# A streaming encoder layer: recurrence inputs between two attention projections, one scaling for both tiles, and the residual kept on chip

## What is computed

```python
h   = LayerNorm_in(x)
P   = h @ w_in          # [RWKV-7 r | k | v | w-lora | a-lora | g-lora] [diff-attn q | k | v]
m   = concat(RWKV7_group(P_rw), DiffAttn_group(P_da)) @ w_out
h   = LayerNorm_1(alpha*h + m)
h   = LayerNorm_2(alpha*h + PEER(h))
# PEER, per block of 128 frames: top 16 keys of two halves, top 16 of their sums, then
u = take(u_tab, idx); act = gelu(einsum('thed,td->the', u, xb))
v = take(v_tab, idx); out = einsum('the,thed->td', gate * act, v)
# a head of attention ends with
o = o * rsqrt(mean(o*o) + eps) * da_subln_g * (1 - lam_init)
```

## Time and profile before

| | |
|---|---|
| median of 3 runs | 4598.03 us (4596.55 to 4604.55) |
| profiled execution, its own time | 4561.83 us |
| its span, first to last instruction | 4560.0 us |
| busy in the span | PE 58%, DVE 56%, POOL 52%, PEld 33%, ACT 16% |
| moved by DMA | 1335.83 MB, 293 GB/s over the span |
| chain that ended last | PE 23%, DVE 22%, POOL 19%, DMA 13%, issue 12% |

### The profile page before, as it was taken

One profiled execution on the slowest core, in us unless ns is written; L12 is line 12 of the kernel. 1 busy time (PEld: TensorE's weight loads), 2 busy tenths in 40 slices (PEclk: granted clock), 3 DMA queues, 4 the chain that ended last, 5 costly groups with the idle time before them and its releaser, 6 DMA issues.

```text
span 4560.0 us, 49804 instructions
## 1 busy us (share of the span) xinstructions
PE 2627.3 (58%) x18687; PEld 1514.2 (33%) x18687; DVE 2574.5 (56%) x5971; ACT 723.9 (16%) x1806; POOL 2365.5 (52%) x2204
## 2 busy tenths in 40 slices
PE   6767356665735666665636776667345544374345
PEld 4546344433502333334303443345112222140001
DVE  3332987756875545656955554657844546573411
ACT  3332023320101122220001222211001111000000
POOL 0000035556465555556556564565666666667665
PEclk8778677777857778667767787868565666665668
DMA  3112267889888788789789888798898998999997
GB/s 119 40 55 89 85 250 252 287 303 365 339 310 331 292 310 309 286 299 367 296 321 366 315 289 294 290 359 344 300 350 330 367 364 329 370 366 334 371 369 304
DMA packets 374663, 1335.83 MB, mean 293 GB/s; under 512 B 40764, under 2 KB 73816, under 8 KB 364184
## 3 DMA queue, kind: packets, MB, share of 16 engines
q0 software_dynamic: 315888, 1150.17, 67.8%
q1 hardware_dynamic: 58536, 182.48, 10.7%
HBM read 1312.29 MB, written 20.20 MB: 292 GB/s over the span
## 4 chain that ended last, share of the span: by engine, by line
PE 23%; DVE 22%; POOL 19%; DMA 13%; issue 12%; another core or an unknown queue 7%; ACT 4%; DVEq 0%; ACTq 0%; SPq 0%; POOLq 0%
POOL ring_u L728 10%; POOL ring_v L728 9%; DMA ring_v<-in_peer_v,idx_t 8%; PE pm L1031 7%; PE pm L1045 6%; DVE ring_u L1388 6%; PE pacc L1073 5%; DMA ring_u<-in_peer_u,idx 4%; DVE arena L1639 1%; DVE arena L1642 1%; DVE arena L1640 1%; PE pm L1256 1%; DVE arena L1641 1%; DVE arena L1638 1%
## 5 line engine op out<-in xcount | busy, mean ns | idle before, releaser
L728 POOL DMA_INDIRECT ring_u<-in_peer_u,idx x1088 | 1196.7, 1100 | 875.9 <-DVE dots L1388 564.0
L1388 DVE CUSTOM_DVE_ANT_0 ring_u<-ring_u,h 128x1024 f32<-128x1024 f32 x1088 | 1297.9, 1224 | 606.0 <-DMA ring_u<-in_peer_u,idx 534.6
L728 POOL DMA_INDIRECT ring_v<-in_peer_v,idx_t x1032 | 1102.1, 1068 | 718.4 <-PE pacc L1073 400.8
L1073 PE MATMUL pacc<-ring_v,spread_w 128*32 128x512 f32 x4128 | 834.0, 892 | 997.1 <-DMA ring_v<-in_peer_v,idx_t 884.4
L1073 PEld LDWEIGHTS pacc<-ring_v,spread_w 128*32 128x32 f32 x4128 | 141.1, 137 | 1385.8 <-issue 1367.4
L1031 PE MATMUL pm<-hT,wts 128*128 128x256 f32 (+1 forms) x2400 | 544.5, 388 | 57.5 <-SPq L654 26.8
L1045 PE MATMUL pm<-arena 64*64 64x64 f32 (+1 forms) x6256 | 388.7, 266 | 287.9 <-issue 90.8
L1031 PEld LDWEIGHTS pm<-hT,wts 128*128 128x128 f32 x2400 | 454.6, 210 | 198.1 <-issue 97.4
L1045 PEld LDWEIGHTS pm<-arena 64*64 64x64 f32 x6256 | 323.9, 167 | 447.5 <-issue 191.0
L771 POOL DMA_DIRECT2D h<-h_scratch x10 | 5.9, 596 | 551.2 <-DVE gates L1628 551.2
L1031 PE MATMUL pm<-wts,hT 128*128 128x384 f32 (+1 forms) x576 | 194.4, 496 | 0.0
(11 more groups left out here) (226 smaller groups left out, 2827.1 us busy)
## 6 DMA issues: line engine op xcount, KB each, us to landing
wts<-in_sets SPq DMA_DIRECT2D x75, 1536.0 KB
ring_u<-in_peer_u,idx POOLq DMA_INDIRECT x1088
ring_v<-in_peer_v,idx_t POOLq DMA_INDIRECT x1032
wts<-in_sets SPq DMA_DIRECT2D x10, 1024.0 KB
h_scratch<-arena SPq DMA_DIRECT2D x16, 512.0 KB, 4.2
arena<-in_subkeys SPq DMA_DIRECT2D x5, 1024.0 KB
arena<-in_x_prompt SPq DMA_DIRECT2D x8, 512.0 KB, 11.2
out<-arena SPq DMA_DIRECT2D x64, 64.0 KB
```

Of the source, the lines that this page charges most:

```text
L728: pool.indirect_dma_start(out=out, out_offset=None, in_=table, in_offset=bass.IndirectOffsetOnAxis(ap=index.bitcast(U32), axis=0)).then_in ...
L1073: x = pe.matmul(pacc[out, c, :], spread_w[:, blocks % 2, quad, place % EIGHTH, :], row[:, c * 512:(c + 1) * 512], start=(place == 0), stop ...
L1388: x = v.tensor_tensor_reduce(ring_u[:, row, :], ring_u[:, row, :], h1[:, g % 3, :], 1.0, 0.0, ALU.mult, ALU.add, dots[:, slot:slot + 1])
```

## The change

**Order in a pair.** The attention's qkv step is cut in two, one per tile. The first stands behind the recurrence's raw step, the second behind decay, and rope behind grams; the other attention steps are spread over the rest of the pair:

```diff
+        qkv = [0, 2][:s.tiles] + [3]
...
-        places = [0, 1, 2, 3] + [3 + (late - 3) * (i + 1) // (len(a) - 4) for i in range(len(a) - 4)]
+        rest = len(a) - len(qkv)
+        places = qkv + [3 + (late - 3) * (i + 1) // rest for i in range(rest)]
...
-        steps = [("qkv", 4, 0.5), ("rope", 1, 1.5)]
+        steps = [("qkv", 4 / s.tiles, 0.5 / s.tiles)] * s.tiles + [("rope", 1, 1.5)]
```

```diff
+            def raw_row(s, j, x, bank):
+
+                k = set_number("rwkv", s, j)
+                pe.wait_ge(S[f"w{k % 2}"], weights_in(k))
+                dense(pm[:, bank, 0:s.width], lambda n: column(k, x)[:, n, :], lambda n: hT[:, n, 0:s.width]).then_inc(S["raw_full"], 1)
...
+                        elif j + 1 < NJ:
+                            raw_row(s, j + 1, *RAW[0])
                         yield "mean"
                         tl.next(S["ysq_ready"])
                         pe.matmul(pm[:, 1, 0:w], mean2[:, :], sq[:, 0:w], start=True, stop=True).then_inc(S["var_full"], 1)
                         leave(pe, "pe")
+                        if not s.last and j + 1 < NJ:
+                            raw_row(s, j + 1, *RAW[1])
                         yield "variance"
...
+                        tl.next(S["ysd"])
+                        if j + 1 < NJ:
+                            raw_row(s, j + 1, *RAW[2])
```

**Both tiles' outputs together.** The root mean squares, the scaling, the turn and the copy are made once for both tiles at the end of the head; PE waits at tile 1 for `o_read`, no longer for the turned and copied output of tile 0:

```diff
-            act.activation(rms[0:r], ss[0:r], ACT.Sqrt, bias=eps_ln[0:r, :], scale=1.0 / P).then_inc(S["rms_ready"], 1)
...
+                        act.wait_ge(S["o_read"], attn_tiles(s, j) + s.tiles)
+                        act.activation(rms[0:r, 0:s.tiles], ss[0:r, 0:s.tiles], ACT.Sqrt, bias=eps_ln[0:r, :], scale=1.0 / P).then_inc(S["rms_ready"], 1)
+                        yield "scale"
```

```diff
-                                    x = dense(pm[0:s.rows, 2 * t + n // 4, (n % 4) * P:(n % 4 + 1) * P], lambda k: mixT[:, k, sl(s, t)],
-                                              lambda k: column(k0, n % 3)[:, k, :])
+                                    out = pm[0:s.rows, 2 * t + n // 4, (n % 4) * P:(n % 4 + 1) * P]
+                                    dense(out, lambda k: mixT[:, k, sl(s, t)], lambda k: column(k0, n % 3)[:, k, :], True)
+                                    x = pe.matmul(out, hT[:, n, sl(s, t)], scaled[:, :], start=False, stop=True)
```

More of the change, by code:

```diff
@@ L430, in build @@
         xt = carve(NCH, CH)
-        p1s = carve(HD)
-        us = carve(HD)
-        s_out = carve(HD)
+        p1s, us, s_out = (rkk[:, i * HD:(i + 1) * HD] for i in range(3))
         keysT = carve(SEQ)
@@ L643, in _ @@
                             sp.dma_start(ln2[:, i, :], ins[name][0].partition_broadcast(P)).then_inc(S["late_in"], 16)
-                    for t in range(s.tiles):
-                        tl.next(S["h_ready"])
-                        sp.dma_start(h_d[t * P:t * P + s.rows, :], x_in[0:s.rows, t, :]).then_inc(S["h_stored"], 16)
-                    tl.next(S["h_stored"], 16 * s.tiles)
                     sp.sem_inc(S["bar_sp"], 1)
@@ L695, in _ @@
                         load_set(base + i + 2)
-                    for t in range(s.tiles):
-                        tl.next(S["h_ready"])
-                        g = s.first_tile + t
-                        sp.dma_start(h1_d[g * P:g * P + s.rows, :], x1[0:s.rows, t, :]).then_inc(S["h1_stored"], 16)
-                    tl.next(S["h1_stored"], 16 * s.tiles)
+                    if s.sample:
+                        sp.wait_ge(S["h_ready"], 2 * len(TILES))
+                        sp.dma_start(h1[s.rows:2 * s.rows, s.first_tile % 4, :], h1[0:s.rows, s.first_tile % 4, :]).then_inc(S["h1_twin"], 16)
                 elif kind == "query":
@@ L759, in store @@
                 r = slice(seg.start + t * P, seg.start + t * P + seg.rows)
-                pool.dma_start((y_s if seg.sample else y_p)[0, r, :], h1[0:seg.rows, g % 3, :]).then_inc(S["y_stored"], 16)
+                pool.dma_start((y_s if seg.sample else y_p)[0, r, :], h1[0:seg.rows, g % 4, :]).then_inc(S["y_stored"], 16)
             for kind, g, arg in order:
@@ L845, in mixing @@
                             yield "tile"
+                        if s.n > 0:
+                            for t in range(SEGMENTS[s.n - 1].tiles):
+                                turned(SEGMENTS[s.n - 1], t)
                         for x in range(2):
@@ L1024, in _, with dense @@
             pe.wait_ge(S["consts"], 1)
-            pe.wait_ge(S["const_in"], 16)
+            pe.wait_ge(S["const_in"], 32)
             pe.sem_inc(S["bar_pe"], 1)
-            def dense(out, lhs, rhs):
+            def dense(out, lhs, rhs, more=False):
                 for k in range(KT):
-                    x = pe.matmul(out, lhs(k), rhs(k), start=(k == 0), stop=(k == KT - 1))
+                    x = pe.matmul(out, lhs(k), rhs(k), start=(k == 0), stop=(k == KT - 1 and not more))
                 return x
@@ L1258, in mixing @@
                             yield "probs"
-                            tl.next(S["o_ready"])
-                            pe.transpose(pm[:, 4, P:P + r], o_s[0:r], ident[0:r, 0:r]).then_inc(S["oT_full"], 1)
-                            yield "out"
+                        tl.next(S["o_read"])
+                        yield "scale"
+                        tl.next(S["o_ready"])
+                        for t in range(s.tiles):
+                            x = pe.transpose(pm[:, 4, P + t * P:P + t * P + r], qk[0:r, t, 0:P], ident[0:r, 0:r])
+                        x.then_inc(S["oT_full"], 1)
+                        yield "out"
                         tl.next(S["oT_read"])
@@ L1520, in mixing @@
                         enter(v, "dve", kind, s, j)
-                        yield "qkv"
+                        for t in range(s.tiles):
+                            yield "qkv"
                         for t in range(s.tiles):
```

197 lines of the change are left out of this document (103 added, 94 removed).

## The result

The changed kernel takes **4445.57 us** (median of 4 runs, 4432.29 to 4459.47) against 4601.29 us (4 runs, 4596.55 to 4604.60): a ratio of 0.9663, 95% interval 0.9631 to 0.9694. That is 156 us less; the forecast was 219 less, 4380 us. The profiled execution of the changed kernel is the slowest of its four (4459.47 us, span 4457.4), that of before was faster than all its timed runs. So the two traces differ by 103 us only. The same kernel run again in another job gave 0.9669 (0.9626 to 0.9712), with a profiled execution of 4405.86 us, so two rounds, 800 to 950 us together, differ by up to 27 us between two profiles of one kernel (rounds 0 and 1: 833 and 806). I read segment 0, which repeats within 0.2 us, from single traces, and all stages with gathers from both profiles and from the medians.

What follows compares the result with a forecast made beforehand. Mixing was taken to hold the gathers back in rounds 2 to 5, with segment 0 uncovered. Segment 0's 67 us, 39, 53 and 53 for segments 1 to 3 and 7 for the sample make 219: 4598 to 4379 us, range 4300 to 4520.

Steps and rivals of the forecast that it cites:

- The front, 15 us for each transition: Segment 0, from one pair's tail to the next pair's last product before the Gram matrices: 15 us less, bounds 11 to 17.
- the clock's rival: Raw rows and projections cut into pieces run at the lower clock; 4.2 us a pair come back, 4464 us; chance 0.13.
- Pair 0, 12 us: Segment 0's first pair: rows start earlier and decays no longer wait for both tiles' q, k, v; 12 us less.
- Project, 2 us longer: Segment 0's projection: 16 more matmuls of 0.29 us, two fewer DVE additions of 1.22 us; 2 us longer.
- One scaling and the tables, 3 us a pair: Pairs of two tiles: three fewer ACT table loads and one scaling round trip less; 3 us a pair, 0 to 4.5.
- some tenths: Front of a pair: rotations, now behind the products and partly beside the Gram matmuls, give back some tenths of a us.
- The share of 0.66 for loaded pairs: Pairs beside gathers: 0.66 of a chain's cut shows, so 18 us become 12 a pair, bounds 0 and 18.
- that is what the gathers can do: Round 8, gathers only: DMA 98% busy at 373 GB/s, taken as what the gathers can do.
- gathers hide the front: Rival: only segment 0 and the saved bytes show, 67 + 8 us, giving 4523 us; chance 0.14.
- The full cut: Rival: all 18 us show in each loaded pair of two tiles, 299 us in all, giving 4299 us; chance 0.12.
- PE's queue as the bound: Rival: raw rows ahead of v pieces in PE's list delay them, 148 us lost, giving 4671 us; chance 0.05.
- Scratch tensors, 2 us a round: Stores and loads of about 18 MB go, 2.1 MB a round; 2 us a round less where DMA is the bound.

Runs made afterwards that it cites:

- the short raw rows: Changed kernel with raw rows late and, in segments 1 to 4, one matmul instead of eight per raw row: 4399.01 us, 0.9644 of the kernel before.
- The places: Changed kernel with the attention's steps put back in their old places, both tiles' q, k, v in one step: 0.984 of the kernel before.
- halved pieces: Changed kernel with each ring piece of u rows given back to POOL in two halves: 3984.54 us, 0.9361 of the kernel before on that chip.

## Why the prediction came out as it did

The sign and the range were right, and the time was 66 us too low, 4380 for 4445.57. Segment 0 gave more than I had put down and the rest about half: 156 measured, less 78 in segment 0, leaves 78 where I had 152. That the total came within 66 us is in part luck: 11 us too little in segment 0 stand against 74 too much beside the gathers.

**The front, 15 us for each transition: right.** From the mean's matmul to the last product the three fell by 16.2, 16.4 and 15.7 us. The first raw row took some 5 us at a granted clock that averaged 0.55 from 99.0 to 104.5, the next two 7.17 together at 1.00; I had 5.5 and 6.8:

```profile
99.00:104.50 5.50, 4.92 (x18) 3.90 (x15) 0.84 (x2) 0.60 (x2) 0.00 (x0) 0.55 0.00 0
106.00:114.00 8.00, 7.89 (x38) 6.30 (x36) 6.01 (x13) 1.54 (x4) 0.00 (x0) 1.00 0.00 0
```

So the clock's rival didn't come: one row of three ran mostly at 1.2 GHz, as a part of it had before (0.68), and the projections after it took 5.32 us a tile, nearly as before (10.48 for both). Over the span the granted clock was 0.736 after 0.726.

**Pair 0, 12 us: 15.3,** its last product at 61.3 instead of 76.6. **Project, 2 us longer: 2.1,** from the last mixT of segment 0 to the list, 174.3 after 172.2.

**One scaling and the tables, 3 us a pair: two sizes that cancel.** From the last product to the mean's matmul the four pairs of segment 0 fell by 4.3, 3.7, 5.5 and 3.0 us, 16.5 where I had 12, nearly as if the term were right. But with each tile scaled by itself this stretch is 43.7 us in pair 1, where it is 36.5 with the change and was 40.2 before. One scaling is thus worth 7.2 there (5.6 to 7.2 in the four pairs), more than my upper bound of 4.5, and the rest of the change gives 3.5 back there, for which I had "some tenths". What I hadn't costed is that PE at tile 1 no longer waits until tile 0's output is scaled, turned and copied; that this makes the difference isn't tested apart from the tables. Of the load itself the rows show 1.283 us and no idle time behind it: in the transition above the load that begins at 120.78 is over when the square root starts at 122.07. The drain of the Trainium skill, page "ScalarE: Activation LUTs", section "What ACT_TABLE_LOAD costs", is not seen in this trace. Segment 0 in all: 67 forecast; 48 for the transitions, 15 for pair 0, 17 for the four stretches behind the products, less 2 for the projection, make the 78 measured.

**The share of 0.66 for loaded pairs: the term that was too large.** It came from segment 2's pairs against the sample's. That difference holds other things than PE's work: one tile instead of two, with DVE busy 254 us instead of 317 and ACT 73 instead of 132. The direct test, the short raw rows, takes PE work alone off the front of each loaded pair and finds about a quarter; and early raw rows in these segments are worth nothing that shows. The places, which do pay there (80 - 28 = 52 us by the medians, some 4 a loaded pair), and one scaling (58 - 27 = 31) pay by something else than the length of the front, if they pay: both numbers are uncertain by 25 us and more. By the traces the pairs of segment 2 fell from 588 to 560 and 552 us, those of segment 3 from 586 to 581 and 568, where I had 48 less in each: 12 a pair became 1 to 9. Rows for the two segments in the changed kernel, against the 588 us of the earlier trace rows:

```profile
1394.00:1954.00 560.00, 373.58 (x3121) 208.40 (x3120) 314.61 (x620) 114.12 (x299) 331.75 (x303) 0.79 0.84 311
2340.00:2921.00 581.00, 395.90 (x3185) 222.42 (x3185) 321.30 (x621) 119.94 (x303) 330.28 (x305) 0.77 0.83 306
```

**Behind it a wrong premise: "that is what the gathers can do".** I had read 373 GB/s in round 8 as the limit of DMA, and 830 of 986 us as what the bytes need. The bytes don't set the rounds: halved, the rounds stay. In round 8 POOL's 192 gathers and the gaps between them fill some 250 of its 280 us; rounds 2 to 5 are 256 gathers, 320 us at least and some 355 at their mean, plus the waits for pieces. So the "gathers hide the front" rival (4523) had a part of the truth: 4445.57 lies about midway between it and the forecast, and what the gathers cost there goes by their number, not their bytes. The full cut (4299) is far off. That rival's sum has a slip: 18 us in each of the four pairs of segment 1 with the 3, 2 and -2 beside them would be 75, not 66. PE's queue as the bound (4671) is out: POOL's waits for v pieces fell by 44 us.

**Scratch tensors, 2 us a round.** That term stood on the bytes and falls with them. Measured with the square root's new place it gave 6 us outside segment 0, within what two runs differ by. In segment 0 the square root's place gave some 12, for which I had no term of its own.

**Not forecast.** In pair 0 of segment 1 PE stands 7 us for the attention's weights, which are asked for only at the barrier and are now needed earlier:

```profile
550.07 7.58 PE L1031 MATMUL pm<-wts,hT 128*128 128x384 f32 x16 [7.04 <-DMA wts<-in_sets]
```

I named these weights for segment 0 and costed them at nothing for the others. Asking for them earlier wasn't tried.

**Open.** Which part of a gather sets the pace beside the mixing: POOL's issue, the DMA engines' time or the way back of a ring piece. How the 52 us of the places beside the gathers come about: the waits for v pieces fell by 44 us in all, and which step lets a piece go sooner isn't isolated. Nor is the gain of halved pieces apart from the chip.

## What to carry to other kernels

When one queue issues small transfers in order, write its time out first: transfers x (time of one + gap) + its waits. A cut elsewhere shows there only as shorter waits. But such a sum always adds up; which part is the bound comes only from runs that cut one part at a time, and from whether the waits take the cut back. Giving buffers back in smaller parts is worth a try, against the same kernel on the same chip. A high busy share of the DMA engines doesn't say that bandwidth is used up (0.84 went with 187 GB/s here and 0.83 with 311): halve the bytes, then the number, and see which one moves the time. And take the share of a cut that will show from an experiment or a stretch that differs by that alone, not from two stages that differ in much else.

## What the runs showed that I had not expected

- 64 rows or 128 rows of 4 KB in a gather: the same rounds (479 and 482 us against 473 and 473), at 171 and 311 GB/s.
- A gather costs POOL 0.94 us and 0.30 pass to the next one; some take 1.7 to 2.0.
- Chips differ: the kernel before takes 4553 to 4601 us on some and 4254 on one. On that one the list of the changed mixing came at 475.7 us, elsewhere at 475.3 and 475.5, so the difference lies beside the gathers.
- A gather of 64 rows instead of 128 keeps the DMA engines busy 1.17 us instead of 1.42: half the bytes, 18% less of their time.
- The norm's square root ahead of the exponentials went with 20 table loads fewer and pairs of segment 0 that were 2 to 5 us shorter, though it wasn't undone alone.
